# Down projection of the last layer: quarters of its weights loaded at other places among the raw weights' loads

## What is computed

```
for i in range(DEPTH):
    ...
    h = rmsnorm(x, norm_ffn[i])
    x = x + jnp.square(jax.nn.relu(h @ w_up[i])) @ w_down[i]
return rmsnorm(x, norm_final)
```

## Time and profile before

| | |
|---|---|
| median of the runs | 1813.27 us |
| profiled execution | 1813.32 us |
| its span | 1811.5 us |
| TensorE, matmuls | 1776.8 us busy, 98% |
| VectorE | 1114.1 us, 62% |
| ScalarE | 834.3 us, 46% |
| GpSimd | 336.4 us, 19% |
| DMA over the span | 127 GB/s |

### The profile page before, as it was taken

One profiled execution on the slowest core, in us unless ns is written; L12 is line 12 of the kernel. 1 busy time (PEld: TensorE's weight loads), 2 busy tenths in 40 slices (PEclk: granted clock), 3 DMA queues, 4 the chain that ended last, 5 costly groups with the idle time before them and its releaser, 6 DMA issues.

```text
span 1811.5 us, 24680 instructions
## 1 busy us (share of the span) xinstructions
PE 1776.8 (98%) x9586; PEld 1449.5 (80%) x9586; DVE 1114.1 (62%) x1763; ACT 834.3 (46%) x1593; POOL 336.4 (19%) x404
## 2 busy tenths in 40 slices
PE   7999999999999999999999999999999999999998
PEld 7767898888888877878878787767788998888886
DVE  7556643233345787887768746677556357574847
ACT  5346532222224555554555644554434445352535
POOL 1403000000000046254462640000020012112120
PEclk9999999999999999999999999999999999999999
DMA  7212333332322453352433444233443248849482
GB/s 256 72 58 63 101 110 116 93 93 93 94 93 75 152 143 128 119 149 97 160 131 123 142 147 164 86 105 118 139 151 130 69 148 189 236 101 259 117 206 70
DMA packets 140419, 230.85 MB, mean 127 GB/s; under 512 B 27264, under 2 KB 59456, under 8 KB 139664
## 3 DMA queue, kind: packets, MB, share of 16 engines
q1 hardware_dynamic: 118944, 166.70, 29.0%
q0 software_dynamic: 20496, 60.10, 12.5%
q10 hardware_dynamic: 864, 2.49, 0.3%
HBM read 216.54 MB, written 12.71 MB: 127 GB/s over the span
## 4 chain that ended last, share of the span: by engine, by line
PE 80%; DVE 11%; ACT 3%; DMA 3%; issue 2%; POOL 1%; SPq 0%; DVEq 0%; ACTq 0%; POOLq 0%
PE m L2135 14%; PE m L2137 13%; PE m L2136 13%; PE m L2146 6%; PE m L2148 6%; PE m L2147 6%; PE s L2298 4%; DVE lo L1396 3%; DMA raw<-in_w_up_dram 2%; PE m L2245 2%; PE m L2244 2%; PE m L2243 2%; PE s L2294 1%; PE m L2270 1%; PE m L2272 1%
## 5 line engine op out<-in xcount | busy, mean ns | idle before, releaser
L2135 PE MATMUL m<-hH,hi 128*128 128x512 f32 (+1 forms) x1392 | 529.4, 380 | 3.2 <-DVE hL L1426 1.8
L2137 PE MATMUL m<-hH,lo 128*128 128x512 f32 (+1 forms) x1392 | 509.1, 366 | 0.0
L2136 PE MATMUL m<-hL,hi 128*128 128x512 f32 (+1 forms) x1392 | 508.3, 365 | 0.0
L1396 DVE TENSOR_TENSOR lo<-raw,hi 128x1024 fp32r<-128x1024 f32 x267 | 335.8, 1269 | 189.7 <-ACT hi L916 189.4
L916 ACT ACTIVATE hi<-raw 128x1024 fp32r<-128x1024 f32 x267 | 276.1, 1050 | 200.8 <-DMA raw<-in_w_up_dram 52.9
L2135 PEld LDWEIGHTS m<-hH,hi 128*128 128x128 f32 x1392 | 262.6, 189 | 47.7 <-DVE hL L1426 2.4
L2137 PEld LDWEIGHTS m<-hH,lo 128*128 128x128 f32 x1392 | 262.4, 189 | 43.4
L2136 PEld LDWEIGHTS m<-hL,hi 128*128 128x128 f32 x1392 | 262.9, 189 | 39.0
L2146 PE MATMUL m<-hi,hH 128*128 128x512 f32 (+1 forms) x320 | 133.8, 418 | 1.6 <-DVE lo L1396 1.6
L2148 PE MATMUL m<-hi,hL 128*128 128x512 f32 (+1 forms) x320 | 122.5, 383 | 0.0
L2147 PE MATMUL m<-lo,hH 128*128 128x512 f32 (+1 forms) x320 | 122.4, 382 | 0.0
(11 more groups left out here) (330 smaller groups left out, 3032.6 us busy)
## 6 DMA issues: line engine op xcount, KB each, us to landing
raw<-in_w_in_dram SPq DMA_DIRECT2D x72, 512.0 KB, 3.6
wq<-in_w_down_dram POOLq DMA_DIRECT2D x40, 512.0 KB, 10.0
hn<-scr_cs_dram POOLq DMA_DIRECT2D x32, 512.0 KB, 4.1
raw<-in_w_up_dram SPq DMA_DIRECT2D x32, 512.0 KB, 5.7
wq<-in_w_down_dram SPq DMA_DIRECT2D x24, 512.0 KB, 7.7
raw<-in_w_gate_dram SPq DMA_DIRECT2D x44, 256.0 KB, 2.8
raw<-in_w_up_dram SPq DMA_DIRECT2D x44, 256.0 KB, 3.1
raw<-in_w_down_dram SPq DMA_DIRECT2D x22, 512.0 KB, 4.2
```

The source lines that it names most:

```text
L1396: e.tensor_tensor(d, r, h.bitcast(F32), ALU.subtract).then_inc(s_lo, 1)
L2135: e.matmul(bank, wh[:, kk, c], h[:, k, q], start=k == 0, stop=False)
L2136: e.matmul(bank, wh[:, kk, c], l[:, k, q], start=False, stop=False)
L2137: x = e.matmul(bank, wl[:, kk, c], h[:, k, q], start=False, stop=k == kt - 1)
```

## The change

Two tables get other numbers:

```
-FS_D_AT = when([s0(f"fs{f}") + s for f in range(NFF2) for s in (-30, -24, -22, -2, -1, 2)])
+FS_D_AT = when([s0(f"fs{f}") + s for f in range(NFF2) for s in ((-30, -22, -10) if f else (-20, -14, -8)) + (0, 4, 8)])
...
-WQ_BEFORE = {BLK[f"up{2 * f}"].u0 + u: (f, i) for f in range(NFF2) for i, u in enumerate((3, 4, 5, 6) if f else (8, 9, 10, 11))}
+WQ_BEFORE = {BLK[f"up{2 * f}"].u0 + u: (f, i) for f in range(NFF2) for i, u in enumerate((2, 4, 5, 7) if f else (5, 6, 7, 8))}
```

## The result

| | before | changed |
|---|---|---|
| median of 4 runs | 1813.24 us (1812.24 to 1813.41) | 1825.0 us (1822.94 to 1825.89) |
| profiled execution | 1813.32 us | 1825.77 us |
| its span | 1811.5 us | 1824.0 us |

The ratio is 1.0064, with a 95% interval of 1.0047 to 1.0082: slower by 11.8 us. The forecast was 1827.8 us in a range of 1817.5 to 1835.5.

The account below looks back on a forecast made before the run. The prediction took TensorE (PE), busy 98% of the 1811.5 us span, as the bound. 1813.3 + 7.8 (pass 0's wait) + 1.7 (low clock) + 5.0 (passes 1 to 3) = 1827.8 us, range 1817.5 to 1835.5.

Parts of the forecast that it names:

- POOL's table: FS_D_AT on POOL: instructions keep their order and waits, so the adding DMAs go as now; cost nothing.
- Pass 0's wait: Before up1: unit 242, ninth load behind the transposes' wait, lands at 1503.4, so PE starts 7.8 us late.
- the landing: Unit 242 in pass 0: lands an estimated 0.2 us after its queue's bytes are through, at 1503.4.
- my 0.11: SP's queue q1 in pass 0: 0.11 MB/us while the first adding pair runs, in place of 0.40.
- The page's fit of bytes over 436 GB/s: Rival without stall, pass 0: by 2.0 us plus bytes over 436 GB/s nine loads land at 1495.2; 1813.3 us, chance 0.05.
- The clock: PE resuming after pass 0's wait finds the clock at 0.50 (1.2 GHz); 1.7 us lost.
- my upper end: Low clock after pass 0's wait: at most 7.8 us at 0.50, so 3.9 us lost.
- Passes 1 to 3: One extra load in each burst makes the eighth raw load late: 1.0 + 2.0 + 2.0 = 5.0 us.
- a sign of being wrong: Passes 2 and 3: the prediction is wrong if PE's waits for fa stay at 0.8 us, not 2 to 3.
- My 1.0 us for pass 1: Pass 1: the eighth raw load's 2.0 us of lateness costs PE about 1.0 us.
- Pass 0 alone: Rival: the extra load of passes 1 to 3 disappears in the idle stretch; 1813.3 + 9.5 = 1822.8 us, chance 0.16.
- my own two terms for pass 0: Pass 0: PE's wait before up1 of 7.8 us and the low clock after it of 1.7 us.

Follow-up runs that it names:

- experiment 1: Only POOL's table FS_D_AT changed, against the kernel before: 1814.09 us against 1812.84, ratio 1.0002.
- experiment 2: Only pass 0's quarters moved, against the kernel before: 1824.62 us, ratio 1.0062.
- experiment 9: Pass 0 as in the changed kernel, but the last quarter of passes 1 to 3 behind all eight raw loads: 1823.36 us, ratio 1.0057.
- experiment 4: The changed kernel, with POOL's first adding pair of pass 0 also waiting until unit 242 has landed: 1818.67 us, ratio 1.0031.
- experiment 5: The changed kernel with 34 unused matmuls of 512 columns added ahead of up1, inside PE's wait: 1827.38 us, ratio 1.0077.
- experiment 10: The kernel of experiment 9 with 34 unused matmuls added inside pass 0's wait: 1821.74 us, ratio 1.0045.
- experiment 3: Only the quarters of passes 1 to 3 moved, against the kernel before: 1813.69 us, ratio 1.0008.
- experiment 11: Only the first quarter of passes 1 to 3 moved ahead of the third raw load, against the kernel before: 1814.88 us, ratio 1.0009.
- experiment 12: Only the last quarter of passes 1 to 3 moved behind the seventh raw load, against the kernel before: 1813.26 us, ratio 1.0002.
- experiment 6: The kernel of experiment 4 with 11 unused matmuls of 512 columns added ahead of up1, inside its wait: 1818.41 us, ratio 1.003.

## Why the prediction was right

**POOL's table** was costed at nothing, and is nothing (experiment 1).

**Pass 0's wait: forecast 7.8 us; 9.4 in the changed kernel's profile, 8.1 in experiment 2's, 8.6 in experiment 9's.** Every step of the chain is there: nine loads behind one wait, unit 242 ninth, its conversion ahead of the ReLUs, 2.4 us to PE. Experiment 2 puts the loss there, and experiment 4 shows that the adding pair's share is what makes it long. In the changed kernel's profile the size is 1.6 us off. Told by events, I let the adding pair run as in the earlier trace rows, issued 7.4 us after the first quarter and landed 13.2 us later, with unit 242 0.4 us behind. Here the pair is issued 8.1 us after the first quarter (1483.81 to 1491.92) and lands 14.5 us later (1506.39; in experiment 2 14.2 us, 1489.14 to 1503.30), and unit 242 with it (in experiment 2 1.7 us behind it). That is 0.7 + 1.3 - 0.4 = 1.6.

Told by bytes, the mis-sized term is the landing. q1's bytes from the first quarter's issue to 1502.88, and to unit 242's landing at 1506.39:

```profile
q1 hardware_dynamic: 2438, 4.72, 72.0%
...
q1 hardware_dynamic: 2875, 5.56, 71.0%
```

The nine loads' 4.72 MB were through 19.1 us after the first quarter's issue, where I had 20.9. But unit 242 landed 3.5 us behind them, not 0.2, which makes up the 1.5 us between 21.05 and 22.6. By then q1 had also moved 0.84 MB more than the nine loads hold, which can only be loads that stand behind it in the queue: some of its packets came later than those of the loads that follow it. In experiments 2, 5, 9 and 10 it landed 1.1 to 2.2 us behind the 4.72 MB. With this order unit 242 lands 21.0 to 22.9 us after the first quarter's issue in the five profiles: the term is 0 to 1.8 us too small from one execution to another. q1's bytes in 1490 to 1496 and in 1497 to 1505 of the changed kernel:

```profile
q1 hardware_dynamic: 1156, 2.23, 103.4%
...
q1 hardware_dynamic: 561, 1.08, 40.4%
```

In the second window POOL's queue moved 1.02 MB, so that each queue had about 0.13 MB/us and both together 0.26, where q1 alone has 0.40: the adding DMAs take more from the load queue than the bytes that they move. At 0.135 MB/us q1 even does better than my 0.11. The rule of the Trainium skill on turns between queues (DMA: Bandwidth & Descriptors, "Queues, rings and completion order") fits the even shares. The page's fit of bytes over 436 GB/s, which is for single DMAs issued by GpSimd and gave no wait, does not hold here: 0.135 MB/us is a third of that, and with the adds kept away too (experiment 4) unit 242 landed 16.4 us after the first quarter's issue, where the fit gives 12.8.

**The clock: forecast 1.7 us**, a middle between two ends; 1.55 in the profile, 1.6 between experiments 9 and 10. The value was near by luck. Experiment 4's profile had 2.9 us after a shorter wait, so the cost does not grow with the wait as my upper end had it. Nor is it the same in every execution: of the changed kernel's four, the two slower ones have a mean granted clock of 0.995 and the two faster ones (1824.23 and 1822.94 us) 0.997. That the clock falls to 1.2 GHz when PE goes without work is what the Trainium skill says too (TensorE: Matmul & The Clock Gate, "Part 1: The HAM clock gate"), and the profile agrees, with 0.50 from 1502 us on.

**Passes 1 to 3: forecast 5.0 us, measured 0 to 3.** This term failed, and with it a sign of being wrong that the prediction named came true: the waits for `fa` in passes 2 and 3 stayed, at 0.7 and 0.4 us. A part of the extra load does stay on the backlog, as forecast: q1 moved 1.03 MB in 1642.33 to 1646.33, against 0.70 in the same stretch of before (1630 to 1634), so that 0.19 of the 0.52 MB were left. But its price was wrong. The eighth load of pass 2 lands 34.8 us after the pass's first quarter (1674.09 - 1639.25) against 34.6. Pass 2's first quarter and its third and fourth raw loads in SP's queue, then the sixth to eighth conversions, a ReLU and PE's waits in pass 2:

```profile
1639.25 3.24 SPq L811 DMA_DIRECT2D wq<-in_w_down_dram  x2
1642.53 1.69 SPq L798 DMA_DIRECT2D raw<-in_w_up_dram  x2
...
1663.56 1.06 ACT L916 ACTIVATE hi<-raw 128x1024 fp32r<-128x1024 f32 x1 [3.48 <-DMA raw<-in_w_up_dram]
1664.85 1.07 ACT L916 ACTIVATE hi<-raw 128x1024 fp32r<-128x1024 f32 x1 [0.22 <-DMA raw<-in_w_up_dram]
1671.33 0.60 ACT L1024 ACTIVATE fa<-m 128x512 f32<-128x512 f32 x1 [0.76 <-PE m L2137]
1674.09 1.06 ACT L916 ACTIVATE hi<-raw 128x1024 fp32r<-128x1024 f32 x1 [2.16 <-DMA raw<-in_w_up_dram]
...
1676.47 0.19 PEld L2135 LDWEIGHTS m<-hH,hi 128*128 128x128 f32 x1 [0.17 <-DVE fa L1504]
1678.20 0.19 PEld L2135 LDWEIGHTS m<-hH,hi 128*128 128x128 f32 x1 [0.51 <-DVE fa L1504]
```

I priced 0.26 MB at q1's rate beside two adds. But the end of the eighth load is not set by q1's bytes. In 1654 to 1662 of the earlier trace rows q1 moved only 0.35 MB at 13% of the engines, far from the 39.7% that it gets when it has work everywhere. In the last 5 us before the landing it moved 0.13 MB before and 0.19 MB in the changed kernel. So a few late packets among the adding DMAs seem to set the landing, with room beside them for the rest of the moved load. I saw that tail and took it only as a reason for the lower price. Which packets they are, and why they are late, the runs don't show. That the moves cost little is what experiments 3, 11 and 12 bear out, within 2 to 3 us. My 1.0 us for pass 1 was too much even by the rows I had: 2.0 us later its eighth load would still have stood 0.3 us earlier in the pass than pass 2's does, which costs 0.8 us there.

**The rivals.** "Pass 0 alone" (1822.8 us, 0.16) is nearest to what happened. By the profile the loss is 9.4 + 1.55 = 10.9 us, and 11.8 between the medians; the 0.9 us between them may be scatter or passes 1 to 3. My sum had 14.5: up to 1.6 too few in one term and 2 to 5 too many in another, which partly cancelled. That the total lies near the forecast is in part luck; this rival had passes 1 to 3 right, and its 9.5 us are my own two terms for pass 0.

## What to carry to other kernels

Before a load is moved in an in-order queue, list the waits that it then stands behind, and look on its consumer's engine at what stands behind its conversion: here three raw loads that nobody waited for got behind a wait, and four ReLUs behind the last of them. Take the rate of a queue for the stretch in which the load will run, with what other queues do then; it was 0.40 MB/us alone and 0.11 to 0.14 beside accumulating DMAs. A load's landing can trail its queue's bytes, here by 1.1 to 3.5 us. In one profile a wait of 3 us on TensorE cost another 3 us in clock, so count waits and their clock together.

## What the runs showed of the hardware that was not expected

- After 3 us without work (experiment 4's profile) the low clock cost 2.9 us, after 9 us it cost 1.55 and, in experiment 2, after 8 us, 2.3 (1556.95 - 1507.34 = 49.61 us against 47.33). The rise came 5.7, 3.1 and 4.6 us after PE resumed, and half of each is the cost. It is no function of the wait's length alone.
- Matmuls on data already there kept the clock at 1.00 through the wait in the profiles of experiments 5, 6 and 10. Without them the changed kernel and experiments 2, 4 and 9 had 0.50 behind it.
- The same instructions gave 1.7 and 0.2 us of waits for `fa` in two executions, and with one order of pass 0 the landing of unit 242 varied from 21.0 to 22.9 us after the first quarter's issue.
- While a load queue and accumulating DMAs both had work, each moved about 0.13 MB/us, together 0.26, where the load queue alone moved 0.40.
